# A decoder layer on one core: three of the four row tiles of the second attention turned in 32x32 blocks instead of by TensorE

## The chip, the cores and the metric

One core of a Trainium2 chip runs the whole layer. The metric is the device time of one execution in microseconds (us); less is better. The kernel before was timed three times: 284.06, 284.39 and 284.71 us, median 284.39.

## The reference, cut to what matters

The layer takes 512 rows of 1024 values, makes all projections of them in one product, runs two causal attentions on the result, gates both, multiplies the joined result with `w_out`, adds the residual and normalises each row.

```python
h = x @ w_in[l]
(qa, ka, va, ga, iq, ik, iw, c_q, c_kv, k_rope, gb) = _split_cols(h)
...
o_a = _dsa_branch(qa, ka, va, iq, ik, iw) * jax.nn.silu(ga)          # 8 heads of 64, 128 chosen keys a row
o_b = _mla_branch(c_q, c_kv, k_rope, q_norm_g[l], w_uq[l], kv_norm_g[l],
                  w_ukv[l], positions) * jax.nn.silu(gb)              # 8 heads, 96 for scores, 64 for values
out = jnp.concatenate([o_a, o_b], axis=-1) @ w_out[l]
x = _layernorm(DEEPNORM_ALPHA * x + out, ln_g[l], ln_b[l])
# inside _mla_branch, for each block of 128 queries:
s = jnp.where(causal[None, None], s, -jnp.inf)
p = jax.nn.softmax(s, axis=-1)
o = jnp.einsum('bhts,bshd->bthd', p, v)
```

Only the second attention (`_mla_branch`), the last product and the row norm are touched here.

## The kernel before, in words

Each engine runs a list of instructions in order, and the engines meet at semaphores. The 512 rows are four row tiles of 128, taken in the order 3, 2, 1, 0 (`ORDER`); "tile i" below means the i-th in that order, so tile 0 has 512 keys before the causal mask ends, tile 1 has 384, tile 2 has 256 and tile 3 has 128. One unit u is one head of one row tile: units 0 to 31 are the first attention, 32 to 63 the second (32 to 39 tile 0, 40 to 47 tile 1, 48 to 55 tile 2, 56 to 63 tile 3).

Per unit of the second attention TensorE (PE) makes the scores (`scores`), VectorE (DVE) scales and masks them and finds the row's largest (`mask_unit`, L1150), ScalarE (ACT) takes the exponential and the row sum (`exp_unit`, L881), and DVE takes the reciprocal of the sum two units later (`normalise_b`, L1190). Then the probabilities have to be turned, keys on the partitions, before they can be multiplied with the values. There are two ways. By TensorE: DVE multiplies with the reciprocal (L1192), PE turns 128 x 128 pieces into PSUM (`transposes`, L1560), ACT copies them to SBUF (`copy_probsT`, L900). By blocks, for the tile that `TURNED` names: ACT multiplies with the reciprocal (`scale_b`, L905), DVE turns 32 x 32 blocks (`turn_blocks`, L1200, three units behind), and 16 DMAs between partitions put the blocks in their places (`turn_pT<-turn_st`, L552). Before, only tile 2 goes by blocks. `probs` has four buffers, and a unit's mask waits until the buffer's last user was turned. The score banks are two, so scores of u wait for the mask of u-2.

When a tile's probabilities are turned, PE multiplies them with the values (`outputs`, L1605) into one of two banks, DVE multiplies the result with the gate (`gate_obT`, L1209), ACT writes its high part (`copy_oT_hi`, L917), and DVE or POOL writes the low part (`oT_low`, L443). The last product (`out_products`, L1643) of a tile has 48 steps, in blocks of 12: for the lower half of the depth (the first attention's part) left columns then right columns, then the same for the upper half (the second attention's part). A step of the upper half needs `copy_oT_hi(i, 1)`. Tile 3 has 72 steps, since its right columns are done in two pieces. The steps of the last product are spread between units by hand (`OUT_AT`, `A_HALF_AT`).

The row norm of a tile is seven takes on DVE: two `ln_residual` (L1220, each with its L1226), `ln_stats`, two `ln_centre` (L1237) and two `ln_scale` (L1247), with one small power on POOL (`root`, L709). Tiles 0, 1 and 2 share one buffer `y`. For this reason `ln_residual` of tiles 1 and 2 first waits until the rows of the tile before have been stored:

```python
if b == 0:
    dve.wait_ge(xres_loaded[i % 2], 16 * (i // 2 + 1))
    if 0 < i < TT - 1:
        dve.wait_ge(stored, 32 * i)
```

The stores are issued by SyncE (SP), in the same queue as the loads of the residual rows and the 16 block DMAs. SP's order before is: loads; stores of tile 0; load; the 16 DMAs of tile 2; stores of tile 1; load; stores of tiles 2 and 3. Before, the row norm of tile 1 is spread over the units from 60 on, and DVE does `gate_obT` of tiles 2 and 3 after it.

Of the kernel before, what the change touches and what calls it, by code (L numbers as in the profile page):

```python
# [6 lines left out]
P = 128  # L7
# [13 lines left out]
BANK = 512  # L21
# [5 lines left out]
def build(nc, x, xT, positions, pos_row, freqs, w_in, q_norm_g, w_uq, kv_norm_g, w_ukv, w_out, ln_g, ln_b, out):  # L27
# [58 lines left out]
    TURNED = 2 * TT - 2  # L86
# [35 lines left out]
    def by_blocks(u):  # L122

        return unit(u)[0] == TURNED

# [15 lines left out]
    SPLIT_ORDER = [(0, 0), (0, 1), (1, 0), (1, 1), (2, 0), (3, 0), (2, 1), (3, 1)]  # L141
    OUT_AT = [NU_A + HEADS * (i + 1) + OT_AT + 2 for i in range(TT)]
# [21 lines left out]
    x_res = sb("x_res", 178, [P, 2, D_MODEL])  # L164
    lng = sb("lng", 186, [P, D_MODEL])
    lnb = sb("lnb", 190, [P, D_MODEL])
# [46 lines left out]
    probsT_b = [sb(f"probsT_b{j}", kib, [P, BANK]) for j, kib in enumerate((162, 164, 166, 168, 170, 172, 174, 176, 88, 90, 196, 198))]  # L213


    short_b = [sb(f"short_b{n}", 88 + n / 2, [P, unit(NU - HEADS + n)[3]]) for n in range(HEADS)]
# [10 lines left out]
    small = sb("small", 203, [P, 256])  # L227
# [27 lines left out]
    with ExitStack() as ctx:  # L255
# [4 lines left out]
        def sem(name):  # L260
# [41 lines left out]
        sums_b_ready, scaled_b, blocks_turned, blocks_placed = (sem("sums_b_ready"), sem("scaled_b"), sem("blocks_turned"),  # L302
                                                                sem("blocks_placed"))
# [102 lines left out]
        def copy_free(eng, u):  # L406

            if u < NU_A:
                if last_user(u) is not None:
                    eng.wait_ge(pv_done, HEADS * (last_user(u) // HEADS + 1))  # L410
                return probsT[u][:, :]
            if u >= NU - HEADS:

                eng.wait_ge(pv_done, NU_A + 2 * HEADS)
            elif u >= NU_A + len(probsT_b):
                eng.wait_ge(pv_done, HEADS * ((u - len(probsT_b)) // HEADS + 1))
            return probsT_of(u)

        def probsT_of(u):

            n = u - (NU - HEADS)
            return short_b[n][:, :] if n >= 0 else probsT_b[(u - NU_A) % len(probsT_b)][:, 0:unit(u)[3]]
# [33 lines left out]
        def _(sp):  # L456
# [83 lines left out]
            sp.dma_start(lng[:, :], ln_g.broadcast_to([P, D_MODEL])).then_inc(ln_loaded, 16)  # L540
            sp.dma_start(lnb[:, :], ln_b.broadcast_to([P, D_MODEL])).then_inc(ln_loaded, 16)
            for i in range(2):
                m = ORDER[i]
                sp.dma_start(x_res[:, i, :], x[m * P:(m + 1) * P, :]).then_inc(xres_loaded[i], 16)
            for i, m in enumerate(ORDER):

                if i == 1:
                    sp.wait_ge(blocks_turned, HEADS)
                    sp.wait_ge(pv_done, NU_A + 2 * HEADS)
                    for c in range(4):  # L550
                        for a in range(4):
                            sp.dma_start(turn_pT[SQ * c:SQ * (c + 1), a], turn_st[SQ * a:SQ * (a + 1), c]).then_inc(blocks_placed, 16)  # L552
                for b, cols in enumerate(PIECES[i][0:2]):
                    sp.wait_ge(y_ready, 2 * i + b + 1)
                    sp.dma_start(out[m * P:(m + 1) * P, cols], y_of(i)[:, cols]).then_inc(stored, 16)
                if i + 2 < TT:
                    m2 = ORDER[i + 2]
                    sp.dma_start(x_res[:, i, :], x[m2 * P:(m2 + 1) * P, :]).then_inc(xres_loaded[i], 16)
# [4 lines left out]
        def _(pool):  # L563
# [187 lines left out]
        def _(act):  # L751
# [173 lines left out]
            for u in range(NU + T_LAG):  # L925
# [37 lines left out]
        def _(dve):  # L963
# [174 lines left out]
            def mask_unit(u):  # L1138
# [7 lines left out]
                if by_blocks(u - NPROBS):  # L1146
                    dve.wait_ge(blocks_turned, (u - NPROBS) % HEADS + 1)
# [34 lines left out]
            def normalise_b(u):  # L1182
# [8 lines left out]
                dve.wait_ge(rinv_ready, u - NU_A + 1 - (HEADS if u >= (TURNED + 1) * HEADS else 0))  # L1191
# [20 lines left out]
            def ln_residual(i, b):  # L1212
# [7 lines left out]
                V.scalar_tensor_tensor(out=v, in0=x_res[:, i % 2, cols], scalar=ALPHA, in1=src,  # L1220
# [29 lines left out]
            def ln_schedule(t):  # L1250

                u = OUT_AT[t]
                return [(u + 6, lambda: ln_residual(t, 0)), (u + 8, lambda: ln_residual(t, 1)), (u + 9, lambda: ln_stats(t)),
                        (u + 9, lambda: ln_centre(t, 0)), (u + 10, lambda: ln_centre(t, 1)),
                        (u + 10, lambda: ln_scale(t, 0)), (u + 11, lambda: ln_scale(t, 1))]

            for u in range(NU):
# [28 lines left out]
                if 0 < i < TT - 1 and j == OT_AT:  # L1286
                    gate_obT(i - 1)

            late = [take for at_u, take in ln_schedule(TT - 3) if at_u >= NU]
            for u in range(NU - NORM_LAG, NU):  # L1290
                normalise_b(u)
            for take in late[:-2]:
                take()
            oT_low(V, TT - 1, 0)
            for take in late[-2:]:
                take()
            for t in range(TT - 2, TT):
                gate_obT(t)
            for t in range(TT - 2, TT):
                oT_low(V, t, 1)  # L1300
# [13 lines left out]
        def _(pe):  # L1314
# [239 lines left out]
            def transposes(u):  # L1554
# [3 lines left out]
                             (normalised, u - NU_A + 1 - (HEADS if u >= (TURNED + 1) * HEADS else 0))))  # L1558
# [4 lines left out]
            def outputs(u):  # L1563
                v, m, h, N = unit(u)
                if v < TT:
                    if u % HEADS < HEADS - 1:
                        return
                    if u % BLOCK_UNITS == HEADS - 1:
                        for b in range(2):
                            bank = 2 * (u // BLOCK_UNITS) + b  # L1570
                            pe.wait_ge(acc_read[bank], ACC_LAST[bank])
                        for t in range(TT):
                            wait_tok(pe, G_V, t)

                    for w in (u - 7, u - 6, u - 3, u - 2):
                        v, m, h, N = unit(w)
                        for a in range(2):
                            wait_copied(pe, w + 2 * a)
                        for j in range(m + 1):
                            for a in range(2):  # L1580
                                ins = mm(oa_bank(v)[A_DIM * a:A_DIM * (a + 1), h // 2 * P:(h // 2 + 1) * P],  # L1581
                                         va[:, j, (h + a) * A_DIM:(h + a + 1) * A_DIM],
                                         probsT[w + 2 * a][:, j * P:(j + 1) * P], start=(j == 0), stop=(j == m))
                                if j == m:
                                    ins.then_inc(pv_done, 1)
                    return

                if h < HEADS - 1 or v == NPASS - 2:
                    return

                for w in range(u - (2 * HEADS if v == NPASS - 1 else HEADS) + 1, u, 2):
                    v, m, h, N = unit(w)
# [3 lines left out]
                    if v == TURNED:  # L1596
                        if h == 0:
                            pe.wait_ge(blocks_placed, 16 * 16)
                    else:
                        for a in range(2):  # L1600
                            wait_copied(pe, w + a)
                    for j in range(m + 1):
                        for a in range(2):
                            pT = turn_pT[:, :, h + a, j] if v == TURNED else probsT_of(w + a)[:, j * P:(j + 1) * P]
# [14 lines left out]
            def out_products(i, a, z):  # L1619
# [3 lines left out]
                for n in range(a, z):  # L1623
# [8 lines left out]
                    if first:  # L1632
# [112 lines left out]
```

## Time and profile before

| what | us |
|---|---|
| median of three runs | 284.39 |
| the profiled execution, its own time | 284.04 |
| its span, first to last instruction | 282.2 |
| PE busy in it | 273.8 |
| DVE busy in it | 232.2 |
| POOL busy in it | 188.6 |
| ACT busy in it | 149.6 |

The profiled execution's time is 1.84 us above its span, which lies around the instructions. All times in rows are us from the span's start unless marked ns. PE works without a longer pause until 275.25; what follows is the last row norm and the last store. Busy time of matmuls is the time from start to a modelled end, and they overlap; the cost of one in a row of many is the distance between starts.

### The profile page before, as it was taken

Reading aid. Unit: us, or ns where it says so; the run is one execution under the profiler, and the core shown is the slowest. Engines: PE = TensorE matmul, PEld = TensorE weight load, DVE = VectorE, ACT = ScalarE, POOL = GpSimd, SP = SyncE. Lnnn points to the kernel's source line nnn. Section 1 sums busy time; section 2 is a strip of 40 time slices with the busy share of each in tenths; the row PEclk is TensorE's granted clock in tenths of the full one; section 3 lists DMA queues with packets and bytes.
Section 4 is the critical chain, followed back from the end, with each engine's and each line's share of the span. In section 5 each row is a group of like instructions: output and inputs, shape, how many; then the busy total and the mean of one; then the engine's idle time right before and its main releaser. Section 6 shows DMA issues by size and latency. Waiting matters only on the chain.

```text
span 282.2 us, 5134 instructions
## 1 busy us (share of the span) xinstructions
PE 273.8 (97%) x1664; PEld 228.6 (81%) x1664; DVE 232.2 (82%) x528; ACT 149.6 (53%) x352; POOL 188.6 (67%) x209
## 2 busy tenths in 40 slices
PE   8999999999999999999999999999999999999990
PEld 7999987778888888888888888885778788888890
DVE  2699998989999999999984798668694967986375
ACT  5656534674452576224188696777764774552000
POOL 5898999834199999999935993885799923010012
PEclk9999999999999999999999999999999999999996
DMA  7985543222623396221238652817800000545022
GB/s 240 364 256 172 151 138 130 74 77 74 149 59 93 83 250 190 74 74 44 70 91 211 231 141 78 224 53 270 349 2 2 0 1 2 172 110 168 0 77 74
DMA packets 20874, 35.41 MB, mean 125 GB/s; under 512 B 6928, under 2 KB 9488, under 8 KB 20592
## 3 DMA queue, kind: packets, MB, share of 16 engines
q1 hardware_dynamic: 20272, 34.79, 41.0%
q10 hardware_dynamic: 576, 0.29, 0.4%
q8 instruction: 14, 0.23, 0.4%
q14 instruction: 12, 0.10, 0.1%
HBM read 26.69 MB, written 2.10 MB: 102 GB/s over the span
## 4 chain that ended last, share of the span: by engine, by line
PE 96%; DMA 1%; DVE 1%; DVEq 0%; issue 0%; ACT 0%
PE ps L1320 52%; PE ps L1643 16%; PE ps L1560 6%; PE ps L1521 5%; PE ps L1581 3%; PE ps L1605 3%; PE ps L1503 2%; PE ps L1336 2%; PE ps L1506 2%; PE ps L1430 2%; DMA w_raw<-in_w_in 1%; PE ps L1540 1%; PE ps L1616 1%; PE ps L1439 0%; PE ps L1413 0%; DVEq L255 0%
## 5 line engine op out<-in xcount | busy, mean ns | idle before, releaser
L624 POOL TENSOR_TENSOR w_lo<-w_raw,w_hi 128x512 fp32r<-128x512 f32 (+3 forms) x62 | 83.8, 1374 | 17.4 <-ACT w_hi L770 16.8
L770 ACT ACTIVATE w_hi<-w_raw 128x512 fp32r<-128x512 f32 (+3 forms) x62 | 35.9, 595 | 55.2 <-PE ps L1320 51.9
L881 ACT ACTIVATE probs<-probs,small 128x512 f32<-128x512 f32 (+3 forms) x64 | 35.7, 559 | 23.2 <-DVE small L1150 22.8
L1643 PE MATMUL ps<-wo_hi,oT 128*128 128x512 f32 (+1 forms) x144 | 45.4, 388 | 0.0
L1320 PE MATMUL ps<-w_hi,x_lo 128*128 128x512 f32 (+3 forms) x120 | 43.0, 362 | 0.0
L1320 PE MATMUL ps<-w_lo,x_hi 128*128 128x512 f32 (+3 forms) x120 | 42.9, 361 | 0.0
L1320 PE MATMUL ps<-x_hi,w_hi 128*128 128x512 f32 x96 | 38.0, 396 | 0.0
L1320 PE MATMUL ps<-x_lo,w_hi 128*128 128x512 f32 x96 | 37.4, 390 | 0.0
L1320 PE MATMUL ps<-x_hi,w_lo 128*128 128x512 f32 x96 | 37.4, 389 | 0.0
L1320 PE MATMUL ps<-w_hi,x_hi 128*128 128x512 f32 (+2 forms) x84 | 32.1, 382 | 0.0
L1643 PEld LDWEIGHTS ps<-wo_hi,oT 128*128 128x128 f32 x144 | 25.9, 189 | 5.2 <-issue 0.2
L709 POOL TENSOR_TENSOR small<-small 128x1 f32<-128x1 f32 x4 | 3.7, 928 | 35.7 <-DVE small L1231 35.7
L1105 DVE MATCH_REPLACE8 score<-small,score 128x256 f32<-128x256 f32 (+2 forms) x48 | 25.5, 539 | 0.0
L1560 PE MATMUL ps<-ident,probs 128*128 128x128 f32 x144 | 25.2, 275 | 0.0
L1320 PEld LDWEIGHTS ps<-w_hi,x_lo 128*128 128x128 f32 x120 | 22.5, 188 | 2.7
L1320 PEld LDWEIGHTS ps<-w_lo,x_hi 128*128 128x128 f32 x120 | 22.6, 188 | 2.6
L1150 DVE CUSTOM_DVE_ANT_0 probs<-ps,causal 128x128 f32<-128x128 f32 (+3 forms) x40 | 17.7, 443 | 7.4 <-PE ps L1521 4.1
L1102 DVE MAX8 small<-score 128x8 f32<-128x256 f32 (+2 forms) x48 | 23.5, 542 | 0.0
L1560 PEld LDWEIGHTS ps<-ident,probs 128*128 128x128 f32 x144 | 17.5, 140 | 6.9 <-issue 4.2
L1320 PEld LDWEIGHTS ps<-x_hi,w_hi 128*128 128x128 f32 x96 | 18.0, 188 | 4.9 <-ACT w_hi L770 0.7
L1320 PEld LDWEIGHTS ps<-x_lo,w_hi 128*128 128x128 f32 x96 | 18.0, 188 | 3.9
L1320 PEld LDWEIGHTS ps<-x_hi,w_lo 128*128 128x128 f32 x96 | 18.0, 188 | 3.5
(196 smaller groups left out, 631.3 us busy)
## 6 DMA issues: line engine op xcount, KB each, us to landing
w_raw<-in_w_in SPq DMA_DIRECT2D x20, 512.0 KB, 3.6
kaT_swap<-kaT SPq DMA_DIRECT2D x8, 256.0 KB, 3.8
w_raw<-in_w_out SPq DMA_DIRECT2D x4, 512.0 KB, 4.8
wo_early<-in_w_out SPq DMA_DIRECT2D x4, 512.0 KB, 4.8
wo_raw_b<-in_w_out SPq DMA_DIRECT2D x4, 512.0 KB, 4.8
x_res<-in_x SPq DMA_DIRECT2D x4, 512.0 KB, 7.1
x_raw<-in_xT SPq DMA_DIRECT2D x3, 512.0 KB, 6.4
out_y<-y SPq DMA_DIRECT2D x6, 256.0 KB, 2.4
```

The lines of the kernel that those rows point to most:

```text
L624: pool.tensor_tensor(w_lo[:, s, 0:n], w_raw[:, s, 0:n], w_hi[:, s, 0:n], ALU.subtract).then_inc(w_lo_ready, 1)
L770: act.activation(dst, w_raw[:, s, 0:n], ACT.Copy).then_inc(w_hi_ready, 1)
L881: act.activation(probs[:, u % NPROBS, 0:N], probs[:, u % NPROBS, 0:N], ACT.Exp, bias=neg_max[:, u % 8:u % 8 + 1], scale=-1.0, accum_out=ro ...
L1102: step(V.max(top8[:, 8 * j:8 * j + 8], sc))
L1105: step(V.match_replace(out=sc, in_to_replace=top8[:, 8 * j:8 * j + 8], in_values=sc, imm_value=TAKEN))
L1150: V.tensor_tensor_reduce(out=probs[:, u % NPROBS, 0:N], in0=ps_s[:, u % 2, 0:N], in1=bias, scale=-scale, scalar=3.0e38, op0=ALU.add, op1=A ...
L1320: ins = mm(dst, a, b, start=start and j == 0, stop=stop and j == len(pairs) - 1)
L1521: ins = mm(ps_s[:, b, 0:N], qbT[:, h, t], kbT[:, h, 0:N], start=True, stop=True)
L1560: ins = nc.tensor.transpose(bank[:, j * P:(j + 1) * P], probs[:, u % NPROBS, j * P:(j + 1) * P], ident[:, :])
L1581: ins = mm(oa_bank(v)[A_DIM * a:A_DIM * (a + 1), h // 2 * P:(h // 2 + 1) * P], va[:, j, (h + a) * A_DIM:(h + a + 1) * A_DIM], probsT[w + 2 ...
L1605: ins = mm(ps_o[A_DIM * a:A_DIM * (a + 1), i % 2, h // 2 * P:(h // 2 + 1) * P], vb[:, j, (h + a) * V_DIM:(h + a + 1) * V_DIM], pT, start=( ...
L1643: ins = mm(out_ps(i, b), oT[i % 2][:, o, k, :], w[:, wcols], start=first, stop=final)
```

## The change

Tiles 1, 2 and 3 go by blocks, tile 0 alone is turned by TensorE. Each turned tile has its own buffers and its own semaphore for placed blocks. SP issues 11 of the 16 DMAs of tile 1 and ScalarE the other five, one a unit from unit 51 to 55; SP issues all of tile 2; of tile 3 SP issues the first eight and ScalarE the last eight after its unit loop. The steps of the last product stand in a table `FILL`, values are multiplied at the units of `PV_AT` (tile 0 at 44, tile 1 at 56) and after the loop (tiles 2 and 3), with steps of tiles 2 and 3 between. Tile 1's last product goes to the two banks that held turned pieces. The row norm of tile 0 is at the units of `LN_AT[0]`, that of tile 1 wholly behind the loop, after the low part of tile 3 and before `gate_obT` of tile 2. SP's order is new. The core of the diff (left out: new addresses of small buffers, semaphore counts that follow from the counting function, and `outputs` split into `outputs_a`, unchanged, and `outputs_b`):

```diff
-    TURNED = 2 * TT - 2
+    TURNED = (TT + 1, TT + 2, TT + 3)
...
+        return unit(u)[0] in TURNED
+
+    def block_count(u):
+
+        return sum(by_blocks(w) for w in range(u + 1))
...
-    SPLIT_ORDER = [(0, 0), (0, 1), (1, 0), (1, 1), (2, 0), (3, 0), (2, 1), (3, 1)]
-    OUT_AT = [NU_A + HEADS * (i + 1) + OT_AT + 2 for i in range(TT)]
...
+    x_res = [sb("x_res0", 202.75, [P, D_MODEL]), sb("x_res1", 182, [P, D_MODEL])]
...
+    lng = sb("lng", 88, [P, D_MODEL])
+    lnb = sb("lnb", 196, [P, D_MODEL])
...
+    turn_st = {v: sb(f"turn_st{v}", kib, [P, 4, HEADS, ORDER[v % TT] + 1, SQ]) for v, kib in zip(TURNED, (182, 174, 186))}
+    turn_pT = {v: sb(f"turn_pT{v}", kib, [P, 4, HEADS, ORDER[v % TT] + 1, SQ]) for v, kib in zip(TURNED, (162, 162, 190))}
...
+            bank = (ps_s[:, 0], ps_s[:, 1], ps_o[:, 0])[b] if i == TT - 1 else (ps_pT if i == 1 else ps_y)[:, b]
...
+        def place_blocks(eng, v, first, end):
+
+            eng.wait_ge(blocks_turned, block_count(HEADS * (v + 1) - 1))
+            if v < NPASS - 1:
+                eng.wait_ge(pv_done, NU_A + HEADS * (v - TT))
+            for n in range(first, end):
+                c, a = divmod(n, 4)
+                eng.dma_start(turn_pT[v][SQ * c:SQ * (c + 1), a],
+                              turn_st[v][SQ * a:SQ * (a + 1), c]).then_inc(blocks_placed[v], 16)
...
-            for i, m in enumerate(ORDER):
-
-                if i == 1:
-                    sp.wait_ge(blocks_turned, HEADS)
-                    sp.wait_ge(pv_done, NU_A + 2 * HEADS)
-                    for c in range(4):
-                        for a in range(4):
-                            sp.dma_start(turn_pT[SQ * c:SQ * (c + 1), a], turn_st[SQ * a:SQ * (a + 1), c]).then_inc(blocks_placed, 16)
+                sp.dma_start(x_res[i % 2][:, :], x[m * P:(m + 1) * P, :]).then_inc(xres_loaded[i % 2], 16)
+
+            def store_rows(i):
+                m = ORDER[i]
                 for b, cols in enumerate(PIECES[i][0:2]):
                     sp.wait_ge(y_ready, 2 * i + b + 1)
                     sp.dma_start(out[m * P:(m + 1) * P, cols], y_of(i)[:, cols]).then_inc(stored, 16)
-                if i + 2 < TT:
-                    m2 = ORDER[i + 2]
-                    sp.dma_start(x_res[:, i, :], x[m2 * P:(m2 + 1) * P, :]).then_inc(xres_loaded[i], 16)
+
+            load_rows(0)
+            sp.wait_ge(pv_done, NU_A)
+            sp.dma_start(lng[:, :], ln_g.broadcast_to([P, D_MODEL])).then_inc(ln_loaded, 16)
+            sp.dma_start(lnb[:, :], ln_b.broadcast_to([P, D_MODEL])).then_inc(ln_loaded, 16)
+            place_blocks(sp, TT + 1, 0, 11)
+            sp.wait_ge(blocks_placed[TT + 1], 16 * 16)
+            load_rows(1)
+            place_blocks(sp, TT + 2, 0, 16)
+            store_rows(0)
+            load_rows(2)
+            place_blocks(sp, TT + 3, 0, 8)
+            store_rows(1)
+            load_rows(3)
+            for i in (2, 3):
+                store_rows(i)
...
-            for i in range(1, TT - 2):
-                oT_low(pool, i, 1)
-            for i in range(TT):
+            root(0)
+            oT_low(pool, 1, 1)
+            for i in range(1, TT):
...
+                for t in range(TT - 2):
+                    if u == GATE_B_AT[t] + 1:
+                        copy_oT_hi(t, 1)
+                if PLACE_AT <= u < PLACE_AT + 5:
+                    place_blocks(act, TT + 1, 11 + u - PLACE_AT, 12 + u - PLACE_AT)
+            copy_oT_hi(TT - 1, 0)
+            place_blocks(act, TT + 3, 8, 16)
...
             def turn_blocks(u):
-                N, h = unit(u)[3], u % HEADS
-                dve.wait_ge(scaled_b, h + 1)
-                if h == 0:
+                v, m, h, N = unit(u)
+                dve.wait_ge(scaled_b, block_count(u))
+                if h == 0 and v == TT + 2:
                     dve.wait_ge(pv_done, NU_A + HEADS)
-                V.transpose(turn_st[:, :, h].rearrange("p c j t -> p j c t"),
+                if h == 0 and v == TT + 3:
+                    dve.wait_ge(blocks_placed[TT + 1], 16 * 16)
+                V.transpose(turn_st[v][:, :, h].rearrange("p c j t -> p j c t"),
...
+            for u in range(NU, NU + T_LAG):
+                if u - NORM_LAG < NU:
+                    normalise_b(u - NORM_LAG)
+                turn_blocks(u - T_LAG)
             late = [take for at_u, take in ln_schedule(TT - 3) if at_u >= NU]
-            for u in range(NU - NORM_LAG, NU):
-                normalise_b(u)
-            for take in late[:-2]:
+            oT_low(V, TT - 1, 0)
+            for take in late:
                 take()
-            oT_low(V, TT - 1, 0)
-            for take in late[-2:]:
-                take()
-            for t in range(TT - 2, TT):
-                gate_obT(t)
-            for t in range(TT - 2, TT):
-                oT_low(V, t, 1)
+            gate_obT(TT - 2)
+            oT_low(V, TT - 2, 1)
+            gate_obT(TT - 1)
+            oT_low(V, TT - 1, 1)
...
+                        elif i == 1:
+                            pe.wait_ge(gate_a_turned, TT)
+                            wait_copied(pe, NU_A + HEADS - 1)
                         else:
-                            pe.wait_ge(out_ps_read, 2 * i - 1 + b)
+                            pe.wait_ge(out_ps_read, b + 1)
...
             NSTEP = 6 * KT
-            per = NSTEP // HEADS
-            for u in range(NU + PV_LAG):
-                if 2 <= u < NU:
+            for u in range(NU):
+                if u >= 2:
                     scores(u)
-                if 0 <= u - A_HALF_AT < 8:
-                    out_products(0, 3 * (u - A_HALF_AT), 3 * (u - A_HALF_AT + 1))
-                if 0 <= u - OUT_AT[0] - 2 < 6:
-                    out_products(0, 3 * KT + 4 * (u - OUT_AT[0] - 2), 3 * KT + 4 * (u - OUT_AT[0] - 1))
-                if 0 <= u - OUT_AT[1] < HEADS:
-                    out_products(1, per * (u - OUT_AT[1]), per * (u - OUT_AT[1] + 1))
-                if 0 <= u - OUT_AT[2] < 6:
-                    out_products(2, 4 * (u - OUT_AT[2]), 4 * (u - OUT_AT[2] + 1))
+                for i, first, per, a, z in FILL:
+                    n = a + per * (u - first)
+                    if a <= n < z:
+                        out_products(i, n, min(n + per, z))
...
-                    outputs(u - A_PV_LAG)
-                if u - PV_LAG >= NU_A:
-                    outputs(u - PV_LAG)
+                    outputs_a(u - A_PV_LAG)
+                for i in range(TT - 2):
+                    if u == PV_AT[i]:
+                        outputs_b(TT + i)
...
+            out_products(TT - 2, NSTEP // 4, 3 * NSTEP // 8)
             out_products(TT - 1, 0, last_first)
-            out_products(TT - 2, NSTEP // 2, NSTEP)
+            outputs_b(NPASS - 2)
+            out_products(TT - 2, 3 * NSTEP // 8, 3 * NSTEP // 4)
+            outputs_b(NPASS - 1)
+            out_products(TT - 2, 3 * NSTEP // 4, NSTEP)
             out_products(TT - 1, last_first, last_all)
...
-T_LAG, PV_LAG = 3, 5
+T_LAG = 3
...
-HIGH_AT = [35, 50, 57]
+HIGH_AT = [35, 46, 54]
+PV_AT = [44, 56]
+GATE_B_AT = [44, 57]
+PLACE_AT = 51
+LN_AT = [(52, 54, 55, 59, 60, 61, 62), (64, 64, 64, 64, 64, 64, 64)]
+FILL = [(0, 40, 3, 0, 24), (0, 48, 4, 24, 48), (1, 48, 2, 0, 12), (1, 54, 6, 12, 24), (2, 56, 3, 0, 12), (1, 60, 6, 24, 48)]
...
```

## Rows read from the trace of the kernel before

**Rows 1.** The page: busy time of each engine, and the chain's shares by engine.
```profile
PE 273.8 (97%) x1664; PEld 228.6 (81%) x1664; DVE 232.2 (82%) x528; ACT 149.6 (53%) x352; POOL 188.6 (67%) x209
...
PE 96%; DMA 1%; DVE 1%; DVEq 0%; issue 0%; ACT 0%
```
**Rows 2.** Timeline, PE at unit 59 (start us, us, engine, line, operation).
```profile
245.12 0.27 PE L1560 MATMUL ps<-ident,probs 128*128 128x128 f32 x1
...
245.23 0.39 PE L1521 MATMUL ps<-kbT,qbT 96*128 96x128 f32 x2
...
245.69 0.40 PE L1643 MATMUL ps<-wo_lo_b,oT 128*128 128x512 f32 x1
...
245.92 0.40 PE L1643 MATMUL ps<-wo_hi,oT 128*128 128x512 f32 x1
```
**Rows 3.** Windows: us, PE, PEld, DVE, ACT, POOL busy (count), PEclk, DMA, GB/s.
```profile
205.60:214.40 8.80, 8.80 (x45) 6.32 (x43) 8.62 (x23) 6.59 (x18) 8.80 (x13) 1.00 0.01 2
```
**Rows 4.** Groups of ACT and DVE from 190 us on: busy us, mean ns.
```profile
L881 ACT ACTIVATE probs<-probs,small 128x256 f32<-128x256 f32 x10 | 5.0, 505 | 7.1 <-DVE small L1150 7.0
...
L905 ACT ACTIVATE probs<-probs,small 128x256 f32<-128x256 f32 x8 | 4.0, 496 | 0.0
...
L1192 DVE TENSOR_SCALAR probs<-probs,small 128x384 f32<-128x384 f32 x8 | 6.3, 790 | 0.3
...
L1200 DVE STREAM_TRANSPOSE turn_st<-probs 128x256 f32<-128x256 f32 x8 | 3.5, 440 | 0.0
...
L1150 DVE CUSTOM_DVE_ANT_0 probs<-ps,causal 128x128 f32<-128x128 f32 x8 | 2.3, 283 | 1.1 <-PE ps L1521 1.1
...
L1209 DVE TENSOR_TENSOR gate<-ps,gate 128x512 f32<-128x512 f32 x4 | 2.8, 691 | 7.0 <-PE ps L1605 7.0
```
**Rows 5.** Timeline, PE: values of tile 1, and the scores of unit 56.
```profile
231.07 2.84 PE L1605 MATMUL ps<-probsT_b,vb 128*64 128x128 f32 x48
...
238.72 0.39 PE L1521 MATMUL ps<-kbT,qbT 96*128 96x128 f32 x2
```
**Rows 6.** Timeline of the DMA issues of SP (SPq) and ACT (ACTq).
```profile
243.88 10.06 SPq L552 DMA_DIRECT2D turn_pT<-turn_st  x16
255.03 1.00 SPq L555 DMA_DIRECT2D out_y<-y  x2
...
278.89 0.38 ACTq L959 DMA_DIRECT2D out_y<-y_last  x1
```
**Rows 7.** DMA issues by line: KB each, median us from issue to landing.
```profile
out_y<-y SPq DMA_DIRECT2D x6, 256.0 KB, 2.4
...
turn_pT<-turn_st SPq DMA_DIRECT2D x16, 64.0 KB, 2.0
```
**Rows 8.** Timeline, row norm of tile 2 on DVE, and one high part on ACT.
```profile
258.25 0.63 ACT L917 ACTIVATE oT<-gate 128x512 fp32r<-128x512 f32 x1 [3.44 <-DVE gate L1209]
...
266.80 0.69 DVE L1220 SCALAR_TENSOR_TENSOR y<-x_res,ps 128x512 f32<-128x512 f32 x1 [1.20 <-PE ps L1643]
...
267.52 0.69 DVE L1226 BATCH_NORM_STATS2 small<-y 128x6 f32<-128x512 f32 x1
...
270.00 1.42 DVE L1247 SCALAR_TENSOR_TENSOR y<-y,small,lnb 128x512 f32<-128x512 f32 x2
```
**Rows 9.** Timeline, PE: values of tiles 2 and 3, then the last products.
```profile
255.51 1.97 PE L1605 MATMUL ps<-turn_pT,vb 128*64 128x128 f32 x32
...
257.28 1.07 PE L1605 MATMUL ps<-short_b,vb 128*64 128x128 f32 x16
...
258.29 0.50 PE L1643 MATMUL ps<-wo_hi,oT 128*128 128x512 f32 x1
...
274.61 0.64 PE L1643 MATMUL ps<-wo_hi,oT 128*128 128x256 f32 x4
```
**Rows 10.** Windows behind PE's last product, columns as in rows 3.
```profile
275.25:277.00 1.75, 0.00 (x0) 0.00 (x0) 1.61 (x6) 0.00 (x0) 0.27 (x1) 1.00 0.00 0
277.00:278.00 1.00, 0.00 (x0) 0.00 (x0) 1.00 (x3) 0.46 (x1) 0.45 (x1) 0.66 0.00 0
```

More of the change, by code:

```diff
@@ L212, in build @@
     oT1 = sb("oT1", 24, [P, 2, KT, P], f32r)
-    probsT_b = [sb(f"probsT_b{j}", kib, [P, BANK]) for j, kib in enumerate((162, 164, 166, 168, 170, 172, 174, 176, 88, 90, 196, 198))]
-    short_b = [sb(f"short_b{n}", 88 + n / 2, [P, unit(NU - HEADS + n)[3]]) for n in range(HEADS)]
+    probsT_b = [sb(f"probsT_b{j}", kib, [P, BANK]) for j, kib in enumerate((162, 164, 166, 168, 170, 172, 174, 176))]
     probs = sb("probs", 16, [P, NPROBS, BANK])
@@ L226, in build @@
     kpe_tok = sb("kpe_tok", 202.5, [P, TT, ROPE_D])
-    small = sb("small", 203, [P, 256])
+    small = sb("small", 206.8125, [P, 256])
     pos_i = sb("pos_i", 204, [P, TT], i32)
@@ L411, in copy_free @@
                 return probsT[u][:, :]
[L412 to L416, printed above, removed]
             return probsT_of(u)
         def probsT_of(u):
-            n = u - (NU - HEADS)
-            return short_b[n][:, :] if n >= 0 else probsT_b[(u - NU_A) % len(probsT_b)][:, 0:unit(u)[3]]
+            return probsT_b[u - NU_A][:, 0:unit(u)[3]]
+        def place_blocks(eng, v, first, end):
[6 more added lines that the diff above has]
+                              turn_st[v][SQ * a:SQ * (a + 1), c]).then_inc(blocks_placed[v], 16)
         def oT_src(i, b):
@@ L1219, in ln_residual @@
                 dve.wait_ge(out_ps_ready, 2 * i + b + 1)
-                V.scalar_tensor_tensor(out=v, in0=x_res[:, i % 2, cols], scalar=ALPHA, in1=src,
+                V.scalar_tensor_tensor(out=v, in0=x_res[i % 2][:, cols], scalar=ALPHA, in1=src,
                                        op0=ALU.mult, op1=ALU.add).then_inc(out_ps_read, 1)
@@ L1250, in ln_schedule @@
             def ln_schedule(t):
[L1252 to L1255, printed above, removed]
+                takes = (lambda: ln_residual(t, 0), lambda: ln_residual(t, 1), lambda: ln_stats(t), lambda: ln_centre(t, 0),
+                         lambda: ln_centre(t, 1), lambda: ln_scale(t, 0), lambda: ln_scale(t, 1))
+                return list(zip(LN_AT[t], takes))
             for u in range(NU):
@@ L1285, in _ @@
                             take()
-                if 0 < i < TT - 1 and j == OT_AT:
-                    gate_obT(i - 1)
+                for t in range(TT - 2):
+                    if u == GATE_B_AT[t]:
+                        gate_obT(t)
+            for u in range(NU, NU + T_LAG):
+                if u - NORM_LAG < NU:
+                    normalise_b(u - NORM_LAG)
+                turn_blocks(u - T_LAG)
             late = [take for at_u, take in ln_schedule(TT - 3) if at_u >= NU]
-            for u in range(NU - NORM_LAG, NU):
-                normalise_b(u)
-            for take in late[:-2]:
+            oT_low(V, TT - 1, 0)
+            for take in late:
                 take()
-            oT_low(V, TT - 1, 0)
-            for take in late[-2:]:
-                take()
-            for t in range(TT - 2, TT):
-                gate_obT(t)
-            for t in range(TT - 2, TT):
-                oT_low(V, t, 1)
+            gate_obT(TT - 2)
+            oT_low(V, TT - 2, 1)
+            gate_obT(TT - 1)
+            oT_low(V, TT - 1, 1)
             for t in range(TT - 2, TT):
@@ L1557, in transposes @@
                 pe.wait_ge(*((probs_ready, u + 1) if u < NU_A else
-                             (normalised, u - NU_A + 1 - (HEADS if u >= (TURNED + 1) * HEADS else 0))))
+                             (normalised, u - NU_A + 1)))
                 for j in range(m + 1):
@@ L1561, in transposes @@
                 ins.then_inc(transposed, 1)
[L1563 to L1576, printed above, removed]
-                        for a in range(2):
[L1578 to L1592, printed above, removed]
@@ new lines, in outputs_a @@
+            def outputs_a(u):
+                if u % HEADS < HEADS - 1:
+                    return
+                if u % BLOCK_UNITS == HEADS - 1:
+                    for b in range(2):
+                        bank = 2 * (u // BLOCK_UNITS) + b
+                        pe.wait_ge(acc_read[bank], ACC_LAST[bank])
+                    for t in range(TT):
+                        wait_tok(pe, G_V, t)
+                for w in (u - 7, u - 6, u - 3, u - 2):
+                    v, m, h, N = unit(w)
+                    for a in range(2):
+                        wait_copied(pe, w + 2 * a)
+                    for j in range(m + 1):
+                        for a in range(2):
+                            ins = mm(oa_bank(v)[A_DIM * a:A_DIM * (a + 1), h // 2 * P:(h // 2 + 1) * P],
+                                     va[:, j, (h + a) * A_DIM:(h + a + 1) * A_DIM],
+                                     probsT[w + 2 * a][:, j * P:(j + 1) * P], start=(j == 0), stop=(j == m))
+                            if j == m:
+                                ins.then_inc(pv_done, 1)
@@ L1593, in outputs, with outputs_b @@
+            def outputs_b(v):
+                for w in range(HEADS * v, HEADS * (v + 1), 2):
+                    _, m, h, N = unit(w)
                     i = v - TT
@@ L1595, in outputs @@
                         pe.wait_ge(*((o_ps_read, TURN_RANK.index(A_RANK[i]) + 1) if i < 2 else (ob_ps_read, i - 1)))
[L1596 to L1599, printed above, removed]
+                        if v in TURNED:
+                            pe.wait_ge(blocks_placed[v], 16 * 16)
+                    if v not in TURNED:
                         for a in range(2):
@@ L1684 @@
 LO_LAG = 1
-T_LAG, PV_LAG = 3, 5
+T_LAG = 3
 NORM_LAG = 2
 NPROBS = 4
-OT_AT = 4
 POS_ROWS_AT, Q_TURN_AT, K_TURN_AT = 6, 19, 23
```

30 lines of the change are left out of this document (8 added, 22 removed).

## The prediction

> **What bounds the kernel now.** I read the page first, for which engine the end hangs on: PE is busy 97% of the span and is 96% of the chain that ended last, while DVE has 82%, ACT 53% [rows 1]. Matmuls overlap, so busy time alone doesn't prove that PE is full; the distance between starts does. In the timeline two steps of the last product start 0.23 us apart, and one turn of a 128 x 128 piece takes 0.11 from its start to that of the scores behind it [rows 2]. Against this the skill speaks: the Trainium skill, Perfetto Trace Analysis, "Identifying the Most-Contended Engine", says that matmul busy time is no good measure and that the weight loads' share is; that is 81% here, and by it a fifth of what PE is freed of would be slack. The starts decide for the trace: between units 48 and 56 nearly every distance is the sum of its parts, so I count every PE turn at its full 0.11.
>
> The windows then show where DVE is the tighter one: from 205.6 to 214.4, while POOL is busy throughout, DVE is busy 8.62 of 8.80 us [rows 3]. The DMA queues and the last 30 us I read last, since the change moves work there.
>
> **What is taken off PE.** Tile 1 had 8 units of three turns, tile 3 eight of one: 32 x 0.11 = 3.5 us. Nothing else of PE's work is dropped, steps and value products are only in another order. If all else is hidden, that is the gain.
>
> **What DVE and ACT get.** For tile 1, DVE loses a multiplication of 0.79 us mean and gets a block turn of 384 columns; for tile 3 one of 128. The trace shows only the turn of 256 columns, 0.44 [rows 4]. Bounds for 384 are 0.44 and the multiplication's 0.79; I take 0.57, as a wider mask costs about 0.13 for 128 more columns. For 128 columns bounds are 0.2 and 0.44, I take 0.3. ACT loses a copy of a turned piece and gets a multiplication, both about as long as its exponential (0.50 for 256) [rows 4]. So neither engine gets slower by more than 0.1 us a unit, PE needs 1.35 to 1.75 us a unit up to unit 55, and the cost there is nothing. If the cover is gone (units 40 to 43 under POOL), about 1 us of the gain is lost; I keep that in the range. The later load of the norm's two rows (behind the first attention's values instead of before it) is needed some 40 us afterwards: nothing.
>
> **Tile 1's blocks arrive late.** Before, the scores of unit 56 start at 238.72 [rows 5]. After, PE has by then done 12 steps more (12 x 0.23 = 2.8), not done tile 1's values (-2.8 [rows 5]) and saved 24 turns (-2.6): 236.1. With three steps of tile 2 it wants the values' blocks at 237.0. SP's eleven DMAs are no problem: unit 47 is turned at unit 50, near 226.7, an issue costs 10.06 / 16 = 0.63 us [rows 6], and the last lands 2.0 behind its issue [rows 7], near 235. ACT's five are: one stands behind the exponential and the multiplication of each of units 51 to 55. Scores of unit 55 start 1.74 before those of 56 (one unit: 0.36 + 6 x 0.23), at 234.35; mask, 0.9 later; exponential and multiplication, each 0.5; ACT is 0.4 behind from the high part of tile 2 and its DMA in unit 54. So its last issue starts near 236.5. What an issue costs ACT is between the 0.38 of its one store and SP's 0.63 [rows 6]; I take 0.6. It lands at 238.5. PE waits 1.5 us (bounds 0 and 3.5). Values take 2.8, so scores of unit 57 start at 241.3, where the kernel before had 240.3, but with nine steps (2.1 us) more behind it and eight turns fewer ahead.
>
> **The new chain behind unit 58.** SP may issue tile 2's 16 DMAs when unit 55 is turned, in unit 58. From the scores of 57: 0.39 for the scores [rows 2], then on DVE mask 0.28, turn 0.44, the gate of tile 1 0.69, a reciprocal, mask 0.28, turn 0.44 [rows 4], with small overlaps 2.5 us: 243.8. From there, each on the one before:
> - SP issues 16 DMAs: 10.1 us [rows 6], until 253.9. The last lands at 255.3.
> - only behind them in SP's order stand the two stores of tile 0, whose rows have been ready in `y` since about 249. The second is issued 0.67 later (1.00 for both, 0.33 for one) [rows 6] and lands in 2.4 [rows 7]: 257.0.
> - `ln_residual` of tile 1 waits for just that (`stored`), and DVE is in order. All seven takes of tile 1 then run: 0.72 for each of four residual and statistics operations (266.80 to 267.52), then 0.2 and 0.1 of small ones, and 1.44 and 1.42 for the centre and scale pairs, 6.1 us as tile 2's did up to 271.42 [rows 8]: 263.1.
> - behind them stands `gate_obT` of tile 2, 0.7 [rows 4], then ACT's high part 0.63 [rows 8], with 0.1 of handing over: 264.5.
>
> PE needs that high part at step 24 of tile 2. It gets there much sooner: units 57 to 59 take 3 x 0.9 and 60 to 63 4 x 1.6, to 250.4; 18 steps, 4.1, to 254.6; blocks at 255.3; values of tile 2 1.8 [rows 9]; six steps 1.4: 258.5. **It stands still for 6.0 us.** The queue that this is moved past is the step to look at: before, the stores of tile 0 were ahead of the 16 DMAs, and the gates of tile 2 waited for PE, not PE for them.
>
> From step 24 PE has: what it did from 258.29 to 275.25 [rows 9] less the 12 first steps of tile 3 (2.7), that is 14.3, and values of tile 3, 1.0 [rows 9]: 15.3 us. The places of tile 3's blocks (SP until about 262, ACT until about 259) and the row norm of tile 2 (DVE free from about 270) are in time. The end behind PE's last product stays 282.2 - 275.25 = 6.95. Span: 264.5 + 15.3 + 6.95 = 286.7.
>
> **The clock.** Behind the last product the granted clock is 1.00 until 277.0, and 0.66 on the mean of 277 to 278, so it fell from 2.4 to 1.2 GHz near 277.3, 2 us into the idle time [rows 10]. A pause of 6 us in the middle would let it fall as well. How soon it comes back no row shows, since PE has no matmul at the lower level in this trace. I take that it comes back as late as it fell, 2.4 us at half speed, a loss of 1.2; bounds are 0 (it doesn't fall) and, were all 15.3 us at half speed, 15; I hold the range's end near 3, as ACT or DVE don't slow with it. The Trainium skill, TensorE: Matmul & The Clock Gate, "Part 1: The HAM clock gate", has the clock halved after an idle stretch and given back only after a sustained busy one; the fall agrees with the trace, the return no row shows, and by its figures the loss would be about 1.7 us, an estimate, for a sum 0.5 higher.
>
> Sum: 286.7 + 1.2 = 287.9 of span, and 1.84 around it: **289.8 us**. The profiled execution (284.04) is 0.35 under the median, within what runs differ by, so I don't add it.
>
> **Rivals.**
> *A: all hidden, the PE turns are simply gone.* PE full throughout speaks for it. Against: it needs the store of tile 0 to land before DVE asks for it at 252, while SP is not through the DMAs ahead of it before 253.9. 284.0 - 3.5 = 280.5 us. Faster. The point from which it decides: PE's pause ahead of step 24 under 1 us.
> *B: the store is not what holds DVE.* Were DVE to start tile 1's norm right after the low part of tile 3, at 252.3, it ends at 258.4, the high part of tile 2 is there at 259.8, PE waits 1.3, no fall of the clock: 259.8 + 15.3 + 6.95 + 1.84 = 283.9, no change. For it: SP could be quicker if issues overlapped; the 16 in 10.06 us speak against.
> *C: the same chain, but tile 1's blocks in time.* Then PE has no first wait and all stands 1.5 earlier: 288.3, still slower. This is in the forecast's range.
> *D: worse.* The front part brings nothing (DVE-bound under POOL, 2 us), or the clock stays down longer: 292 to 294.
>
> **How the numbers follow.** Forecast (with C) 0.74, its own range 286.5 to 292; A 0.10, B 0.10, D 0.06. What can be told from no change here is about 0.2%, 0.6 us. Faster: A and a part of B, 0.15; within: 0.06; slower: 0.79. The range leaves out A and the upper half of D and takes in B's value: 283.5 to 292.3.
>
> **What would show it.** In the trace after: no PE turns for tiles 1 and 3; a wait of 1 to 2 us ahead of tile 1's values, with ACT's last DMA as releaser; SP's 16 issues of tile 2 in about 10 us and the stores of tile 0 behind them; DVE idle some 4 us ahead of tile 1's first residual; PE idle 5 to 7 us ahead of an upper-half step of tile 2, released by ACT's high part; granted clock under 1.00 there. It is wrong if the store lands before DVE needs it, if PE's long pause is missing, or if the last product starts before 274.

## The result and the profile after

The changed kernel takes 290.2 us (median of four runs, 289.64 to 291.05), the kernel before 284.24 beside it; the ratio is 1.021, 95% interval 1.019 to 1.023. So it is slower by 6.0 us. The forecast was 289.8, slower.

The page of the profile after: span 288.3, PE busy for 1.1 us less than before and yet 6.1 us more of span [rows 1].

```profile
PE 272.7 (95%) x1632; PEld 226.8 (79%) x1632; DVE 230.9 (80%) x528; ACT 150.6 (52%) x352; POOL 188.0 (65%) x209
...
PE 81%; DVE 8%; SPq 3%; DMA 3%; issue 2%; ACT 1%; DVEq 0%; ACTq 0%
```

The 32 PE turns are gone (1632 matmuls for 1664), and the chain is no longer PE alone: DVE, SP's queue and DMAs have 14% of it. Half of DVE's 8% (`score`, L1101) lies at 47 to 61 us, in the first attention, which the change doesn't touch. What is new lies late. SP's DMA issues show where (start us, us, engine, line, operation):

```profile
227.32 7.22 SPq L425 DMA_DIRECT2D turn_pT<-turn_st  x11
238.06 0.33 SPq L546 DMA_DIRECT2D x_res<-in_x  x1
243.36 10.01 SPq L425 DMA_DIRECT2D turn_pT<-turn_st  x16
253.42 1.08 SPq L552 DMA_DIRECT2D out_y<-y  x2
254.55 0.56 SPq L546 DMA_DIRECT2D x_res<-in_x  x1
255.15 5.23 SPq L425 DMA_DIRECT2D turn_pT<-turn_st  x8
```

Tile 0's stores start at 253.42, behind ten microseconds of issues; in the kernel before they stood ahead of the 16. DVE's timeline after that, with what ended each idle time:

```profile
251.99 0.69 DVE L447 TENSOR_TENSOR oT<-gate,oT 128x512 fp32r<-128x512 f32 x1 [0.21 <-ACT oT L927]
257.23 0.69 DVE L1235 SCALAR_TENSOR_TENSOR y<-x_res,ps 128x512 f32<-128x512 f32 x1 [4.55 <-DMA out_y<-y]
...
261.75 1.41 DVE L1262 SCALAR_TENSOR_TENSOR y<-y,small,lnb 128x512 f32<-128x512 f32 x2
263.08 0.68 DVE L1224 TENSOR_TENSOR gate<-ps,gate 128x512 f32<-128x512 f32 x1
```

DVE stands still for 4.55 us until the store has landed, then makes tile 1's row norm, and only at 263.08 the gate of tile 2, whose values PE had finished long before. PE's timeline:

```profile
238.18 2.84 PE L1615 MATMUL ps<-turn_pT,vb 128*64 128x128 f32 x48 [0.82 <-DMA turn_pT<-turn_st]
...
255.00 1.97 PE L1615 MATMUL ps<-turn_pT,vb 128*64 128x128 f32 x32
256.89 0.50 PE L1656 MATMUL ps<-wo_hi,oT 128*128 128x512 f32 x1
...
264.48 0.79 PE L1656 MATMUL ps<-wo_hi,oT 128*128 128x512 f32 x1 [5.93 <-ACT oT L927]
265.07 0.63 PE L1656 MATMUL ps<-wo_lo_b,oT 128*128 128x512 f32 x1
265.50 0.63 PE L1656 MATMUL ps<-wo_hi,oT 128*128 128x512 f32 x1
```

PE waits 5.93 us for ACT's high part, and its steps then start 0.43 us apart instead of the 0.23 of [rows 2]. The windows around the pause (the seventh column is the granted clock, as in [rows 3]):

```profile
256.89:258.55 1.66, 1.66 (x8) 1.05 (x6) 1.28 (x2) 0.00 (x0) 0.00 (x0) 1.00 0.90 278
258.55:264.48 5.93, 0.00 (x0) 0.00 (x0) 5.10 (x11) 0.63 (x1) 0.99 (x1) 0.67 0.39 126
264.48:267.20 2.72, 2.72 (x6) 2.15 (x7) 0.67 (x1) 0.00 (x0) 0.00 (x0) 0.50 0.76 240
```

Narrow windows at the two edges:

```profile
260.50:260.60 0.10, 0.00 (x0) 0.00 (x0) 0.10 (x1) 0.00 (x0) 0.10 (x1) 0.80 0.53 144
267.30:267.40 0.10, 0.10 (x2) 0.10 (x1) 0.00 (x0) 0.00 (x0) 0.00 (x0) 0.56 0.00 0
```

0.50 is 1.2 GHz. The clock fell near 260.6, 2.0 us into the pause, and came back near 267.4, 2.9 us after PE went on. Some six steps at 0.43 for 0.23 lose 1.3 us.

### The profile page after: what moved, and what is told of

It reads as the page before. It is cut to its first block, busy times and chain, and to the rows that moved or that the text cites. A ratio compares the mean times of both kernels' runs of the same rounds, so it can differ in the third digit from the quotient of the medians.

```text
span 288.3 us, 5076 instructions
## 1 busy us (share of the span) xinstructions
PE 272.7 (95%) x1632; PEld 226.8 (79%) x1632; DVE 230.9 (80%) x528; ACT 150.6 (52%) x352; POOL 188.0 (65%) x209
## 4 chain that ended last, share of the span: by engine, by line
PE 81%; DVE 8%; SPq 3%; DMA 3%; issue 2%; ACT 1%; DVEq 0%; ACTq 0%
PE ps L1335 47%; PE ps L1656 10%; PE ps L1536 4%; PE ps L1575 4%; DVE score L1101 4%; SPq L425 3%; PE ps L1594 3%; PE ps L1615 3%; PE ps L1518 2%; PE ps L1351 2%; PE ps L1521 2%; DMA w_raw<-in_w_in 1%; DMA out_y<-y 1%; PE ps L1555 1%; PE ps L1626 1%
## 5 line engine op out<-in xcount | busy, mean ns | idle before, releaser
L634 POOL TENSOR_TENSOR w_lo<-w_raw,w_hi 128x512 fp32r<-128x512 f32 (+3 forms) x62 | 84.0, 1377 | 17.6 <-ACT w_hi L780 16.8
L1656 PE MATMUL ps<-wo_hi,oT 128*128 128x512 f32 (+1 forms) x144 | 46.5, 393 | 6.1 <-ACT oT L927 6.1
L1101 DVE SCALAR_TENSOR_TENSOR score<-relu,small,score 128x384 f32<-128x384 f32 (+2 forms) x21 | 18.6, 884 | 1.9
L1575 PE MATMUL ps<-ident,probs 128*128 128x128 f32 x112 | 19.1, 276 | 0.0
```

The source lines that it names most:

```text
L634: pool.tensor_tensor(w_lo[:, s, 0:n], w_raw[:, s, 0:n], w_hi[:, s, 0:n], ALU.subtract).then_inc(w_lo_ready, 1)
L1101: V.scalar_tensor_tensor(out=sc, in0=relu[:, i % 4, a * N:(a + 1) * N], scalar=iw[:, m * IDX_HEADS + h:m * IDX_HEADS + h + 1], in1=causal[ ...
L1575: ins = nc.tensor.transpose(bank[:, j * P:(j + 1) * P], probs[:, u % NPROBS, j * P:(j + 1) * P], ident[:, :])
L1656: ins = mm(out_ps(i, b), oT[i % 2][:, o, k, :], w[:, wcols], start=first, stop=final)
```

## The experiments

**e1: the gate first.** DVE makes the gate of tile 2 before tile 1's row norm.

```diff
             oT_low(V, TT - 1, 0)
-            for take in late:
-                take()
             gate_obT(TT - 2)
             oT_low(V, TT - 2, 1)
+            for take in late:
+                take()
             gate_obT(TT - 1)
```

> DVE does the gate and the low part of tile 2 before the row norm of tile 1, nothing else is changed. Theory (the pause stands because the gate is behind the norm, and the norm behind the store): the values of tile 2 end near 256.9 as in the changed kernel, the high part is there at 258.4, PE's pause of 6 us and the fall of the clock are gone, PE ends near 273.9. But the row norms of tiles 1 and 2 now end near 273.2 instead of before the first piece of tile 3 is ready at 271, so the tail is 1.5 us longer: 284.1 us. Rival (the late blocks or the DMAs themselves hold PE, the order on DVE doesn't matter): still 288 to 290.

Measured 284.18 us, ratio to the kernel before 0.9994 (0.9982 to 1.0006). PE's long pause is gone and the clock stays at 1.00. The theory of the pause holds: the gate is early, and the row norms come late. The total came out as expected with two of its parts off.

```profile
257.59 0.69 DVE L1224 TENSOR_TENSOR gate<-ps,gate 128x512 f32<-128x512 f32 x1 [4.31 <-PE ps L1615]
...
272.57 1.42 DVE L1262 SCALAR_TENSOR_TENSOR y<-y,small,lnb 128x512 f32<-128x512 f32 x2
273.91 0.69 DVE L1235 SCALAR_TENSOR_TENSOR ps<-x_res,ps 128x512 f32<-128x512 f32 x1
...
263.05 1.09 PE L1615 MATMUL ps<-turn_pT,vb 128*64 128x128 f32 x16 [1.03 <-DMA turn_pT<-turn_st]
```

DVE idles until the values of tile 2 are there (4.31 us, now released by PE), and later goes from tile 2's norm into tile 3's without idle time, where the changed kernel had 0.69 us of it. But PE ends at 275.58, not at 273.9: this execution runs 0.6 us behind that of the changed kernel from 172 us on, and PE now waits 1.03 us for tile 3's blocks. The tail is 7.4 us, 0.5 longer than before and not 1.5. So of the 3.5 us of turns, 1.8 go into PE's two waits for blocks (0.8 of it ahead of tile 1's values), 0.2 into one for a high part and 0.5 into the tail; some 0.8 more are missing, and where they are isn't shown.

**e2: a buffer of its own for tile 1's norm.** The order on DVE stays; the wait for the store has no reason any more.

```diff
+    y_own = sb("y_own", 4, [P, D_MODEL])
-        return y_last if i == TT - 1 else y
+        return {1: y_own, TT - 1: y_last}.get(i, y)
-                    if 0 < i < TT - 1:
+                    if i == 2:
                         dve.wait_ge(stored, 32 * i)
```

> The row norm of tile 1 writes a buffer of its own (4 KB a partition where the second attention's queries were) and so doesn't wait for the stores of tile 0; the order on DVE stays. Theory (the store is what holds DVE): the norm starts at 252.7 instead of 257.2 and ends at 258.8, the high part comes at 260.2, PE waits 2 us and its clock stays up: 284.6 us. Rival (something else in DVE's queue or in the residual rows holds the norm): unchanged, 290.

Measured 284.53 us, ratio 1.0002 (0.9990 to 1.0014), no change from before. The norm starts as soon as the low part of tile 3 is made, and PE waits 1.3 us where it waited 5.9:

```profile
252.71 0.68 DVE L1236 SCALAR_TENSOR_TENSOR y_own<-x_res,ps 128x512 f32<-128x512 f32 x1
...
258.56 0.68 DVE L1225 TENSOR_TENSOR gate<-ps,gate 128x512 f32<-128x512 f32 x1
```
```profile
259.96 0.50 PE L1657 MATMUL ps<-wo_hi,oT 128*128 128x512 f32 x1 [1.34 <-ACT oT L928]
```

So either link of the chain, cut alone, gives the 6 us back: the store ahead of the norm, or the norm ahead of the gate.

**e3: work in the pause.** 22 matmuls into a free bank, for the clock.

```diff
-            out_products(TT - 2, 3 * NSTEP // 8, 3 * NSTEP // 4)
+            out_products(TT - 2, 3 * NSTEP // 8, NSTEP // 2)
+            pe.wait_ge(ob_ps_read, 2)
+            for _ in range(22):
+                mm(ps_o[:, 1, :], oT1[:, 0, 0, :], wo_hi[:, 0, 0], start=True, stop=True)
+            out_products(TT - 2, NSTEP // 2, 3 * NSTEP // 4)
```

> 22 matmuls of 512 columns into a free PSUM bank are put into PE's pause ahead of step 24 of tile 2, to keep it active; they change no result. Theory (the clock's fall costs the difference between a step each 0.43 and 0.23 us, for the six steps after the pause): granted clock 1.00 throughout, 1.3 us less, 288.9 us. Rival (the pause alone is the loss and the lower clock is not on the path): 290.2. If the added matmuls run past the end of the pause: later by what they overrun.

Measured 288.48 us, ratio 1.0149 (1.0127 to 1.0171). The step behind the pause starts at nearly the same place (264.21 for 264.48), and the granted clock is 1.00 in every window from 250 us to PE's end:

```profile
258.02 5.15 PE L1693 MATMUL ps<-wo_hi,oT 128*128 128x512 f32 x22
264.21 0.50 PE L1656 MATMUL ps<-wo_hi,oT 128*128 128x512 f32 x1 [1.05 <-ACT oT L927]
```

From there to the values of tile 3 it takes 2.95 us (267.16) instead of 4.29 (264.48 to 268.77): 1.34 us, the loss by the clock. The medians differ by 1.7; in the profiled executions 0.3 of it is an earlier front part.

**e5: the stores first in SP's queue, as before.**

```diff
-            place_blocks(sp, TT + 2, 0, 16)
             store_rows(0)
             load_rows(2)
+            place_blocks(sp, TT + 2, 0, 16)
```

> SP issues the two stores of tile 0 (and the load behind them) ahead of the 16 block DMAs of tile 2, as the kernel before had it. Theory (SP's queue is a chain either way): the rows of tile 0 are ready near 249, so the block DMAs start near 250.7 and land near 262; the row norm of tile 1 starts at 252.7 and no longer holds the gate, but PE stands 7 us ahead of tile 2's values, the high part comes at 265.5 instead of 264.4: 291.1 us, within 1 us of the changed kernel. Rival (putting the store behind the DMAs was the whole mistake): 284.

Measured 291.47 us, ratio 1.0246 (1.0221 to 1.0270). The norm starts at 252.61, yet the pause is only moved, to the place where PE wants tile 2's blocks:

```profile
261.86 3.68 PE L1615 MATMUL ps<-turn_pT,vb 128*64 128x128 f32 x32 [6.82 <-DMA turn_pT<-turn_st]
```

PE wants these blocks 6.8 us before they land, and again at the lower clock at first: the values take 3.68 us instead of 1.97. So undoing the order alone repairs nothing. That doesn't mean that stores and block DMAs can't both be early in one queue: in the kernel before they were, with these stores issued ahead of the 16 DMAs that start at 243.88 [rows 6]:

```profile
241.65 1.60 SPq L555 DMA_DIRECT2D out_y<-y  x2
```

In the changed kernel tile 0's last take of the norm ends only at 249.05, because `LN_AT[0]` puts the takes from the first `ln_centre` on at units 59 to 62. With an earlier norm of tile 0 the old order might have cost little; no run tried it.

**e4: 12 and 4.** SP issues 12 of tile 1's block DMAs, ScalarE four, one a unit from 51 to 54.

```diff
-            place_blocks(sp, TT + 1, 0, 11)
+            place_blocks(sp, TT + 1, 0, 12)
-                if PLACE_AT <= u < PLACE_AT + 5:
-                    place_blocks(act, TT + 1, 11 + u - PLACE_AT, 12 + u - PLACE_AT)
+                if PLACE_AT <= u < PLACE_AT + 4:
+                    place_blocks(act, TT + 1, 12 + u - PLACE_AT, 13 + u - PLACE_AT)
```

> SP issues 12 and ScalarE four (units 51 to 54) of tile 1's 16 block DMAs, instead of 11 and five. Theory (PE waits for ScalarE's last issue in unit 55, and all behind unit 58 hangs on that moment): the blocks land near 236.7, PE's wait of about 0.8 us ahead of tile 1's values goes, and the end moves by the same 0.8: 289.4 us. Rival (the wait there is hidden by the long pause later): no change, 290.2.

Measured 290.44 us, ratio 1.0205 (1.0188 to 1.0223): nothing gained, the expectation missed. The trace shows that PE went on 0.63 us sooner (263.85; 0.9 if one counts from the first attention's values, which start 0.3 later in this execution), but the clock came back later. Windows of e4, columns as above:

```profile
257.90:263.85 5.95, 0.04 (x2) 0.01 (x1) 5.12 (x11) 0.63 (x1) 0.99 (x1) 0.88 0.34 110
263.85:269.20 5.35, 5.35 (x12) 3.79 (x12) 0.67 (x1) 0.00 (x0) 0.00 (x0) 0.50 0.39 121
...
262.40:262.50 0.10, 0.00 (x0) 0.00 (x0) 0.10 (x2) 0.00 (x0) 0.00 (x0) 0.61 0.00 0
269.20:269.30 0.10, 0.10 (x3) 0.04 (x2) 0.00 (x0) 0.00 (x0) 0.00 (x0) 0.75 0.00 0
```

The pause is as long (5.95), but the clock fell later in it (mean 0.88 against 0.67), and stayed low for 5.4 us of work instead of 2.9. The stretch at 0.50 is as long in both, 6.8 us (260.6 to 267.4, here 262.4 to 269.2); it began 1.8 us later and so covered more of the work. Twelve slow steps in place of six cost 1.1 us more (5.41 us from the end of the pause to tile 3's values instead of 4.29), and that is more than the earlier blocks had gained.

**e8: e3 and e4 together,** to test that explanation.

> The added matmuls of e3 and the 12 and four block DMAs of e4 together. e4 alone brought nothing, though its blocks landed earlier and PE's pause ended 0.6 us earlier. Theory (there PE's clock stayed at the lower level for 5.3 us after the pause instead of 2.7, which gave back the gain): with the clock kept up the split is worth its 0.6 to 0.8 us: 287.8 us against e3's 288.5. Rival (the split is worth nothing, the long pause absorbs it): 288.5.

Measured 287.47 us, ratio 1.0117 (1.0095 to 1.0140), 1.0 under e3. In the profiled executions the step behind the pause starts 1.03 us earlier than in e3, 0.24 of it from an earlier front part:

```profile
263.18 0.50 PE L1656 MATMUL ps<-wo_hi,oT 128*128 128x512 f32 x1 [0.92 <-ACT oT L927]
```

So the split is worth about 0.8 us once the clock is held up, and with e4's windows that is good evidence that e4 lost it to the clock. It is not more than that: the intervals of e3 and e8 overlap a little, and the clock was read in one execution of each kernel.

**e7: what a PE turn is worth.** The kernel before, with one turn a unit of tile 1 instead of three.

```diff
-                for j in range(m + 1):
+                for j in range(1 if v == TT + 1 else m + 1):
                     ins = nc.tensor.transpose(bank[:, j * P:(j + 1) * P], probs[:, u % NPROBS, j * P:(j + 1) * P], ident[:, :])
```

> The kernel before, in which PE turns only the first of the three 128 x 128 pieces of each unit of tile 1 (two thirds of that tile's probabilities are left unturned); nothing else is changed. It measures what a PE turn is worth. Theory (each costs its full 0.11 us): 16 x 0.11 = 1.8 us less than the kernel before, 282.5. Rival (DVE is the bound in units 40 to 47, or the share of weight loads is right and PE has slack): a gain between 0 and 1.2 us.

Measured 282.53 us against 284.61 beside it, ratio 0.9931 (0.9916 to 0.9946): 2.0 us, with an interval of 1.5 to 2.4, for 16 turns. The full 0.11 us each is in it; slack of a fifth (1.4 us) is just outside.

**e6: the parts that help, together.** e2's buffer, e4's split, and on DVE five takes of tile 1's norm, then the gate and the low part of tile 2, then the last two takes.

```diff
             oT_low(V, TT - 1, 0)
-            for take in late:
+            for take in late[:5]:
                 take()
             gate_obT(TT - 2)
             oT_low(V, TT - 2, 1)
+            for take in late[5:]:
+                take()
             gate_obT(TT - 1)
```

> Own buffer for the row norm of tile 1, 12 and four block DMAs, and on DVE the first five takes of that norm, then the gate and the low part of tile 2, then its last two takes. Theory: the high part of tile 2 is there at 258.0, PE is short of work for 0.4 us, and the norm of tile 2 ends at 270.1, before tile 3's first piece: 282.3 us, faster than both kernels. Rival (a further wait, for the stores of tile 1 or for the blocks of tile 3, takes the pause's place): 284 or more.

Measured 282.87 us, ratio 0.9945 (0.9930 to 0.9959): faster than both. The norm now lies in DVE's idle time, and the gate follows the values at once. PE has no wait ahead of step 24, where 0.4 us was expected, but one for tile 3's blocks, which only the rival had named; apart from 0.2 us for a high part it is the only one:

```profile
261.24 1.10 PE L1618 MATMUL ps<-turn_pT,vb 128*64 128x128 f32 x16 [1.36 <-DMA turn_pT<-turn_st]
```

**e9: tile 3's blocks ahead of the stores.**

```diff
-            store_rows(0)
+            sp.wait_ge(y_ready, 2)
             load_rows(2)
             place_blocks(sp, TT + 3, 0, 8)
+            store_rows(0)
             store_rows(1)
```

> e6 with SP's order changed once more: behind tile 2's block DMAs the load of tile 2's residual rows, then the eight block DMAs of tile 3, and only then the stores of tile 0, which nothing waits for soon now. Theory (in e6 PE still waits 1.4 us for tile 3's blocks, whose last issues stand behind the two stores): the blocks land 1.1 us earlier, 281.8 us. Rival (the norm of tile 2 now waits for the stores, or DVE holds the tail): 282.9 or more.

Measured 281.38 us, ratio 0.9898 (0.9882 to 0.9914), 2.9 us under the kernel before. The waits of PE from 200 us to the end are now these (waits view, all of it):

```profile
PE ps L1660 <- ACT oT L929: 0.2, 1, 0.2
```

## Why the prediction was right, step by step

- *PE's turns are worth 0.11 us each, 3.5 us in all.* Right: e7 measures it for 16, and e9 brings 2.9 us (interval 2.4 to 3.4) of the 3.5 to the end.
- *DVE and ACT get no slower.* Right. The unknown block turns take 577 ns for 384 columns (taken: 0.57) and 308 for 128 (0.3). Beside POOL, DVE got lighter: 7.50 us busy from 205.6 to 214.4 instead of 8.62 [rows 3].
- *Tile 1's blocks come late.* Right in place, too large: scores of unit 56 at 236.29 (236.1), the values at 238.18 instead of 238.5. I had put ACT's last issue behind an exponential and a multiplication of 0.5 us each, and 0.4 for ACT being late, near 236.5. In the trace it starts at 235.94, 0.07 after the exponential and ahead of the multiplication (L915), which stands before it in ACT's list:

```profile
235.87 0.51 ACT L891 ACTIVATE probs<-probs,small 128x256 f32<-128x256 f32 x1 [0.53 <-DVE small L1163]
235.94 0.52 ACTq L425 DMA_DIRECT2D turn_pT<-turn_st  x1
...
236.38 0.49 ACT L915 ACTIVATE probs<-probs,small 128x256 f32<-128x256 f32 x1
```

So PE waited 0.82 us where 1.5 was predicted.

- *The chain behind unit 58.* Right in its links: issues from 243.36 (243.8) for 10.01 us (10.1); norm at 257.23 (257.0), since the second store took 3.1 us to land, not 2.4; gate at 263.08 (263.1); PE on at 264.48 (264.5). That the end fits to 0.02 us is luck: the chain began 0.4 us early (although this execution's front part runs 0.4 behind the one that the rows are from), the store came 0.7 late against that, and norm, gate and high part together were 0.25 shorter. e1 and e2 cut it at two places, and either cut removes the pause.
- *The clock.* It fell 2.0 us into the pause and was low for 2.9 us of work: 1.3 us lost, by e3, against 1.2 taken. That was partly luck. I had assumed 2.4 us at half speed; e4 has 5.4 for a pause of the same length. The Trainium skill, TensorE: Matmul & The Clock Gate, "Part 1: The HAM clock gate", has the clock given back after a sustained busy stretch; by its figure I estimated 1.7 us lost. The traces lie on either side of that estimate: 1.3 us in the changed kernel, about 2.5 in e4 (5.41 us from the end of the pause to tile 3's values, for e3's 2.95).
- *The rest and the tail.* 264.48 to PE's last product at 281.31 is 16.8 us, less 1.3 for the clock 15.5 (15.3); the tail 6.99 (6.95).
- *The rivals.* A (all hidden, 280.5) and B (store not holding DVE, 283.9) did not occur, but e2 makes B true by construction and lands at 284.5, and e9 comes within 1 us of A. C put the split at 1.5 us; e8 against e3 gives 1.0 by the medians and 0.8 by the traces.

Not settled: of the 3.5 us of turns, e9 lacks 0.6, of which one wait holds 0.2. Where the rest lies was not tried.

## What to carry to other kernels

When work moves off a full engine into DMAs, count the issues: here 16 small DMAs are ten microseconds of a queue, and whatever stands behind them in that queue moves back by as much, here a store that nobody seemed to wait for. Follow each moved step until it meets the full engine again: store, buffer free, row norm, gate, product. A buffer shared by two tiles and an order inside one engine's list were the two links, and each could be cut without giving up the change. Where a total comes out right, look at its parts: in e1 and in the long chain, misses of 0.4 to 1 us cancelled. A pause of the matmul engine cost more than its length here (5.9 us and 1.3 by the clock), and small shifts of timing ahead of it could be judged only with the clock held up.

## What the runs showed of the hardware that I had not expected

- After equal pauses (5.93 and 5.95 us) the clock came back after 2.9 us of work in one execution and 5.4 in another, of a kernel whose pause began 0.6 us earlier; the fall moved too, from 2.0 to 4.5 us into the pause. The stretch at 1.2 GHz was 6.8 us long in both, so the later it began, the more work it covered. A time saved ahead of a pause can be lost behind it.
- DMA issues on ScalarE (0.51 to 0.59 us each) ran beside its activations and delayed none that the trace shows; each of the five started 0.06 to 0.15 us after its unit's exponential began, ahead of a multiplication that stands before it in ScalarE's list.
- Matmuls whose result nobody reads made the kernel faster (e3): by 1.3 us in the traces, behind the pause.
